# A delta-rule pipeline: the turn, gate and store of a tile's output one round later, its norm behind the masked products

## The reference

```
# per head, chunks of 64 tokens; g = cumulated log decay inside the chunk
lower = strict_tril((k*beta) k^T * decay);  attn = tril(q k^T * decay)
[u, w] = (I + lower)^-1 [v*beta, k*beta*exp(g)]
for each chunk:                     # the state S goes from chunk to chunk
    v_new = u - w S
    o     = (q*exp(g)) S + attn v_new
    S     = S*exp(g_last) + (k*exp(g_last-g))^T v_new
o_gdn = rms_norm(o, gdn_norm_g) * silu(z)
```

## Time and profile before

| what | value |
|---|---|
| three timed executions | 3395.01, 3401.8, 3408.82 us (median 3401.8) |
| the profiled execution | 3407.16 us, with a span of 3405.7 us |
| mean granted TensorE clock in it | 0.958 of full |
| busy share of the span | PE 91%, DVE 48%, ACT 31%, POOL 33% |
| `delta_rule` rounds | first masked product at 685.0 us, last at 1039.3 us, next stage from 1099 us |

### The profile page before, as it was taken

One profiled execution on the slowest core, in us unless ns is written; L12 is line 12 of the kernel. 1 busy time (PEld: TensorE's weight loads), 2 busy tenths in 40 slices (PEclk: granted clock), 3 DMA queues, 4 the chain that ended last, 5 costly groups with the idle time before them and its releaser, 6 DMA issues. The chain is left out here.

```text
span 3405.7 us, 45425 instructions
## 1 busy us (share of the span) xinstructions
PE 3095.6 (91%) x15074; PEld 2550.6 (75%) x15074; DVE 1641.7 (48%) x2713; ACT 1064.9 (31%) x2363; POOL 1115.6 (33%) x1245
## 2 busy tenths in 40 slices
PE   6999997768887897979879999989998999999898
PEld 5888885557776776868667888878887788887676
DVE  3653005446664554555576545675554433333333
ACT  2111004334434554542233333433333311111321
POOL 2322241165655866620045333453332000000122
PEclk9999998889988998999989999999999999999999
DMA  3212115412223211125624222232221532333433
GB/s 142 78 74 79 69 62 188 157 51 80 70 61 98 60 41 52 30 73 181 220 84 136 74 92 74 75 114 92 74 90 53 176 101 88 101 96 116 150 120 97
DMA packets 284042, 329.32 MB, mean 97 GB/s; under 512 B 32896, under 2 KB 224256, under 8 KB 279552
## 3 DMA queue, kind: packets, MB, share of 16 engines
q1 hardware_dynamic: 238248, 265.84, 24.6%
q0 software_dynamic: 12384, 45.09, 3.8%
q10 hardware_dynamic: 33280, 16.78, 1.7%
HBM read 210.73 MB, written 116.92 MB: 96 GB/s over the span
## 5 line engine op out<-in xcount | busy, mean ns | idle before, releaser
L2107 PE MATMUL ff_bank<-ff_x_hi,ff_w_lo 128*128 128x512 f32 x1240 | 488.2, 394 | 31.9 <-DVE ff_w_lo L2287 22.5
L2108 PE MATMUL ff_bank<-ff_x_lo,ff_w_hi 128*128 128x512 f32 x1240 | 487.0, 393 | 0.0
L2109 PE MATMUL ff_bank<-ff_x_hi,ff_w_hi 128*128 128x512 f32 x1240 | 486.6, 392 | 0.0
L2090 POOL TENSOR_TENSOR ff_w_sum<-ff_w_raw 128x512 f32<-128x512 f32 x210 | 299.3, 1435 | 495.7 <-DVE ff_w_lo L2287 439.3
L299 PE MATMUL in_h_ps<-in_x_hi,in_w_lo 128*128 128x512 f32 x704 | 276.6, 393 | 26.0 <-POOL in_w_lo L255 26.0
L2107 PEld LDWEIGHTS ff_bank<-ff_x_hi,ff_w_lo 128*128 128x128 f32 x1240 | 235.6, 190 | 84.0 <-DVE ff_w_lo L2287 25.3
L2497 PE MATMUL fd_acc<-fd_w_hi,fd_a_lo 128*128 128x512 f32 x704 | 279.8, 397 | 13.2 <-DVE fd_a_lo L2481 13.2
L2499 PE MATMUL fd_acc<-fd_w_hi,fd_a_hi 128*128 128x512 f32 x704 | 278.0, 395 | 0.0
L2498 PE MATMUL fd_acc<-fd_w_lo,fd_a_hi 128*128 128x512 f32 x704 | 278.0, 395 | 0.0
L301 PE MATMUL in_h_ps<-in_x_hi,in_w_hi 128*128 128x512 f32 x704 | 275.8, 392 | 0.0
L300 PE MATMUL in_h_ps<-in_x_lo,in_w_hi 128*128 128x512 f32 x704 | 275.8, 392 | 0.0
(11 more groups left out here) (383 smaller groups left out, 6640.6 us busy)
## 6 DMA issues: line engine op xcount, KB each, us to landing
ff_w_raw<-w_gate_up SPq DMA_DIRECT2D x44, 1024.0 KB, 5.1
scratch_hT<-in_out SPq DMA_DIRECT2D x22, 1024.0 KB, 3.9
fd_a_raw<-scratch_hid SPq DMA_DIRECT2D x176, 128.0 KB, 2.1
dr_qkv<-scratch_hT SPq DMA_DIRECT2D x16, 768.0 KB, 5.2
in_w_raw<-w_in POOLq DMA_DIRECT2D x22, 512.0 KB, 3.9
scratch_hid<-ff_first SPq DMA_DIRECT2D x44, 256.0 KB, 2.3
scratch_hid<-ff_second SPq DMA_DIRECT2D x44, 256.0 KB, 2.3
fd_w_raw<-w_down SPq DMA_DIRECT2D x22, 512.0 KB, 5.3
```

The source lines that it names most:

```text
L2090: pool.tensor_tensor(w_sum[:, SUM_SLOT[m]], w_raw[:, b, one], w_raw[:, b, two], op).then_inc(w_sum_done, 1)
L2107: pe.matmul(acc, w_lo[:, wm, ws], x_hi[:, xm, k], start=first_mm, stop=False, skip_group_check=skip)
L2108: pe.matmul(acc, w_hi[:, wm, ws], x_lo[:, xm, k], start=False, stop=False, skip_group_check=skip)
L2109: return pe.matmul(acc, w_hi[:, wm, ws], x_hi[:, xm, k], start=False, stop=last_mm, skip_group_check=skip)
```

## The change

On TensorE `a_out(t)` no longer ends round t+3. It is called as `a_out(t - 1)` in the middle of the next advancing round, between `s_z(n, 0)` and `a_kv(t, 0)`, and waits for `vb_done` of that count instead. On VectorE `a_gate(t)` moves from the end of its round to behind `a_v(t, 1)` of the next, and `a_norm(t)` moves within its round, from ahead of `p_lower` and `p_attention` to behind them, still ahead of `spread`. On SyncE the store of `mix` and the load of the next gate values come a round later. The last tile's turn, gate and store stand behind the loop. No instruction is added or removed.

```diff
@@ sync
+            def store(t):
+                sp.wait_ge(mix_done, t + 1)
+                dst = mixT[0:HEADS, :, P * t:P * t + P].rearrange("a p t -> p a t")
+                sp.dma_start(dst, mix[:, t % 2]).then_inc(stored[t % 2], 16)
+                if t + 2 < TILES:
+                    load_z(t + 2)
...
-                if t is not None:
-                    sp.wait_ge(mix_done, t + 1)
...
+                if t:
+                    store(t - 1)
+            store(TILES - 1)
@@ tensor
-            def a_out(t, m):
+            def a_out(t):
                 pe.wait_ge(on_done, t + 1)
-                if m is not None:
-                    pe.wait_ge(vb_done, m + 1)
+                pe.wait_ge(vb_done, min(t + 4, TILES))
...
                     s_z(n, 0)
+                if advance and t > 0:
+                    a_out(t - 1)
                 if advance:
                     a_kv(t, 0)
...
                     p_gram_q(m)
-                if advance:
-                    a_out(t, m)
+            a_out(TILES - 1)
@@ vector
                     a_s(t, 0)
                     a_v(t, 1)
+                    if t > 0:
+                        a_gate(t - 1)
...
                     s_z(n, 1)
                     s_u(n, 1)
-                if advance:
-                    a_norm(t)
                 if first:
                     p_lower(m)
                     p_attention(m)
+                if advance:
+                    a_norm(t)
                 if base:
                     spread(e)
-                if advance:
-                    a_gate(t)
+            a_gate(TILES - 1)
```

## The result

The changed kernel takes 3422.8 us (median of seven executions, 3416.4 to 3430.2) against 3396.6 for the kernel before (seven, 3386.2 to 3408.8). The ratio is 1.0076, with an interval of 1.0061 to 1.0090: slower by 26 us, inside the stated range of 3384 to 3446 and 8.8 above the stated 3414. The profiled execution took 3430.2 us with a span of 3428.7, 23.0 more than before, and its mean granted clock is 0.953 where it was 0.958.

What follows compares the result with a forecast made beforehand. Three loops through the start of `L` (GpSimd's block loop, VectorE's late norm, TensorE's) bound the kernel. 3407.2 profiled + 11 for rounds + 1 for ends = 3419, stated as 3414 since the profiled run lay 5.4 above the median; range 3384 to 3446.

Steps and rivals of the forecast that it cites:

- Norm behind the products delays the solve: VectorE, norm ahead of the spread of `U`: solve starts 3.40 us after `L` begins, an added 1.47 us on TensorE's way.
- X: The moment at which VectorE begins `L`, through which all three loops pass; times in a round count from it.
- The new wait equals the old: TensorE: a 2.5 us wait for `U` every round replaces the wait of nearly that length for `on`.
- The undisturbed round: Full round from `L` to `L` without fallen clock or stalls: 3.40 + 18.09 + 0.59 = 22.1 us, against a mean of 24.1.
- Rival 1: TensorE's clock stays up despite the wait: rounds near 22.1 to 22.6 us, time 3378 to 3384; chance 0.15.
- What the shift does to the factors: VectorE's tiny factors begin 14.3 us after `L`, or 15.7 with a fallen clock, then under GpSimd's wide products.
- a disturbed round: Round with fallen clock and factors under GpSimd's products: bounds 23.5 to 29.5 us, taken as 26.0.
- rival 2: VectorE's factors fall under GpSimd's products in nearly every round: 4 to 6 us each, time 3437 to 3452; chance 0.25.
- the traced stall: VectorE factor standing 3.86 us across three GpSimd products; at that length the prediction put a disturbed round at 28.7 us.
- How often: Share of the twelve rounds disturbed: three in four, nine at 26.0 us and three at 22.1, mean 25.0, +11 us.
- Gate and store a round later: Gate, 0.75 us per tile on VectorE, hidden behind its wait for TensorE; SyncE's store and load also cost nothing.
- Ends: Stretches before and after the twelve rounds: the later norm and transposes show once at most, 0 to 2 us, taken as 1.

Runs made afterwards that it cites:

- the kernel with the filled wait: Changed kernel plus sixteen idle identity transposes on TensorE between state product and solve in each advancing round; 3377.5 us, 0.9946 of the kernel before.
- the filled end: Changed kernel plus the sixteen idle transposes only in the three rounds without a tile to prepare; 3408.1 us, 1.0033 of the kernel before.

## Why the prediction came out right, and where it did not

The outcome and the mechanism were right; two sizes were not, and one of them made most of the miss. That 3422.8 came so near to 3414 is in part luck. The step forecast against the kernel before was 12 us and the measured one is 26. The stated time was built on a median of 3401.8 from three executions, 5.2 above that of all seven, and this hid 5 of the missing 14 us.

*Norm behind the products delays the solve.* The start was worked out as X+3.40 and came at X+3.41 in the rounds shown, with the norm directly behind `attnT` and 1.47 us long. Right, and the experiments with the norm alone (24 of 26 us) and with the norm one place later (43 us less) show it to be the cause, the whole of it within the intervals.

*The new wait equals the old.* 2.5 us in each round were stated, 2.43 came. Right.

*The undisturbed round.* 22.1 us were worked out; the one such round took 22.0, and in the kernel with the filled wait all twelve did. Right. Rival 1, the clock holds, was priced at 3378 to 3384. The kernel in which it was made to hold, in the end too, took 3377.5.

*What the shift does to the factors.* They begin at X+15.8, as stated for a fallen clock (X+15.7). The price of a disturbed round was mis-sized: I took 26.0, and the eleven took 25.2 in the mean, six of them only 23.7 to 23.9, near the lower bound of 23.5. This answers rival 2 as well. Its condition, factors later than X+14.6, was met in eleven rounds, and its price of 4 to 6 us against an undisturbed round was not: they cost 3.2. The reason is on GpSimd, in the same round as above:

```profile
864.33 1.29 POOL L1067 TENSOR_TENSOR dr_qdT<-dr_qkv,dr_eg 128x512 f32<-128x512 f32 x1 [0.40 <-ACT dr_eg L1287]
866.02 1.27 POOL L1057 TENSOR_TENSOR dr_dec<-dr_dif,dr_upto 128x512 f32<-128x512 f32 x1 [0.40 <-ACT dr_dif L1293]
```

A slow TensorE also makes ScalarE's exponentials late (L1287 began at X+15.6 here and at X+13.9 in the undisturbed round), and GpSimd waits for them twice. The products start at X+16.3 with a gap of 0.4 us behind the first, in which VectorE goes on, so the factor L1416 stood 1.12 us and not 3.9. In three other rounds, those of 26.6 or 26.7 us, two operations stood 1.3 us each. The long stall of the earlier trace rows came back once, in the round of 797.0, where the products came in one piece:

```profile
813.85 3.86 DVE L1422 TENSOR_SCALAR dr_rnq<-dr_rn 128x4 f32<-128x4 f32 x1
```

```profile
813.98 1.26 POOL L1067 TENSOR_TENSOR dr_qdT<-dr_qkv,dr_eg 128x512 f32<-128x512 f32 x1
815.20 1.25 POOL L1057 TENSOR_TENSOR dr_dec<-dr_dif,dr_upto 128x512 f32<-128x512 f32 x1
816.42 1.25 POOL L1059 TENSOR_TENSOR dr_dec<-dr_dif,dr_below 128x512 f32<-128x512 f32 x1
```

The SBUF page of the Trainium skill ("SBUF — State Buffer", section "SBUF: two separate sides") names as the operations that can stand those of VectorE with two SBUF inputs or in a two-port mode. The runs agree: the spread of `U` with two SBUF operands stood 4.31 us, while `kbg`, which reads PSUM, took 0.68 or 0.69 in every trace. As to length the rows differ among themselves: 4.45 us fall within one product of 4.51, and 3.86 span three, where the page speaks of one instruction. The stall of 3.86 us also began 0.13 us ahead of the first product, by a record that is rough on GpSimd, so that who came first cannot be told from it. The 28.7 us that the prediction gives for the traced stall does not follow from its terms: 17.2 + 3.86 and 7.45, the middle of 6.3 to 8.6, make 28.5.

*How often.* Nine of twelve were taken, eleven came. More rounds were disturbed than stated and each cost less, and by luck the two errors cancel: mean round 25.0 stated, 24.9 measured.

*Gate and store a round later.* Costed at nothing; the kernel with these alone has shorter rounds. Right for the rounds.

*Ends.* This is the term that failed. "0 to 2, I take 1" was worked out from the order of instructions, and 13.4 came. With the clock mostly held, in the filled end, 2.1 were left. What I left out is the very thing that I had priced for the rounds: the clock. In the end TensorE has little to do beside the chain; it waits more (2.4 us for `U`; 3.3 for the state, which stands behind `Z` and so behind ScalarE's preparation of attention; 3.8 for the last `on`), and a fall there lasts longer. The three low stretches that begin in the end were 17.1, 10.2 and 23.9 us, and 47 us of them lie inside it, against 58.0 in all twelve rounds. Two of the waits, VectorE's wait behind the second, and the clock inside the three stretches:

```profile
1051.54 0.44 PE L1154 MATMUL dr_b<-dr_ident,dr_U 128*128 128x128 f32 x2 [2.42 <-DVE dr_U L1451]
...
1082.40 0.76 PE L1183 MATMUL dr_b<-dr_S,dr_wT 128*64 128x128 f32 x5 [3.34 <-DVE dr_S L1482]
```

```profile
1080.56 0.76 DVE L1459 TENSOR_TENSOR dr_Z<-dr_b,dr_corner 128x256 f32<-128x256 f32 x2 [3.78 <-ACT dr_T L1307]
```

```profile
1053.00:1070.00 17.00, 15.78 (x72) 13.83 (x71) 6.10 (x16) 1.15 (x3) 8.19 (x29) 0.50 0.81 193
1083.70:1093.80 10.10, 10.10 (x44) 8.77 (x43) 4.08 (x10) 0.77 (x2) 6.46 (x6) 0.50 0.48 130
1104.20:1123.80 19.60, 9.90 (x44) 7.89 (x41) 4.74 (x13) 6.66 (x17) 10.51 (x11) 0.50 0.11 31
```

With the waits of the end filled, a stretch of 3.4 us came in place of the first two.

By the steps the profiled execution should have taken 3419 and took 3430; the missing 11 are the end's. The end of the kernel before does not explain itself either: among the thirteen kernels the end ran from 61.1 to 75.7 us, and the low clock in it from 9.0 to 46.9.

## What to carry to other kernels

Before moving an instruction down a list, ask what waits for those it is put ahead of: the norm cost least behind the spread, where nothing that stood behind it was needed at once (21.4 us a round), some 1.9 us a round ahead of `L` by the prediction's count, and most ahead of the operand of the next solve (24.9 us a round). In a loop like this one, where TensorE has hardly a gap, price a wait by the slow products behind it, more than by its own length; a filled wait is the cheap experiment that tells the two apart, and a better order makes the filling needless. And price the end of a pipeline like its rounds: its waits are longer, and in this stage a product of 4.5 us on a neighbour engine is only there.

## What the runs showed of the hardware

Filling a wait of 2.4 us with 1.97 us of idle transposes raised the granted clock of the rounds from 0.90 to 1.00, the upper level of 2.4 GHz, and took 35 us off 299. Equal waits did not have equal results: behind one of 2.43 us the clock held at 1.00, behind the next of 2.43 it was 0.51 (1.2 GHz) at once. A second wait of only 1.35 us in a round was followed by the lower clock as well. In the twelve rounds of the changed kernel no low stretch was longer than 6.8 us; at the end of the stage they reached 23.9, and in its first three rounds 17.1. A 128x4 operation of VectorE cost 0.16 us, or 4.45 where GpSimd had begun a product of 4.51 us 0.08 us before it.
